# One set of weights for both directions in the mLSTM heads, and denominators from a product with ones

## The reference

```
w[t,s] = (q[t]·k[s]) * exp(log_d[t,s] - m[t])
num[t] = sum_s w[t,s] v[s]
den[t] = sum_s w[t,s]
h[t]   = num[t] / max(|den[t]|, exp(-m[t]))
```

```python
h = num / jnp.maximum(jnp.abs(den), jnp.exp(-m_t))[..., None]
...
return yc_f + jnp.flip(yc_b, axis=2), yl_f + jnp.flip(yl_b, axis=2)
...
y = from_heads(head_norm(h, LN_EPS, True)) * norm_g + skip * xc
return (y * jax.nn.silu(z.astype(jnp.float32))).astype(z.dtype)
```

## Time and profile before

| | us |
|---|---|
| median of 3 runs | 2862.51 |
| profiled execution | 2845.39 |
| its span | 2843.5 |
| heads: first product of scores to last gating | 2015.0 to 2613.6 |
| PE busy in the whole span | 2487.3 |
| DVE busy in the whole span | 1573.6 |

### The profile page before, as it was taken

How to read it: one execution, slowest core, us unless ns; L and a number is a source line. 1 busy time by engine, 2 the same in 40 slices (tenths; PEclk the granted TensorE clock), 3 DMA queues, 4 the chain that set the end, 5 groups by cost and what they waited for, 6 DMA issues and landing times. The chain is left out here.

```text
span 2843.5 us, 53344 instructions
## 1 busy us (share of the span) xinstructions
PE 2487.3 (87%) x22670; PEld 2117.7 (74%) x22670; DVE 1573.6 (55%) x2510; ACT 901.1 (32%) x1504; POOL 729.5 (26%) x689
## 2 busy tenths in 40 slices
PE   6899999995898986777959999999599999995986
PEld 2577776775877774666848888878499999995865
DVE  3026878644456545764665665566455656565233
ACT  2113344231232333555123333332443443431310
POOL 1111110115757642000222222221222222221421
PEclk8999999997999997889979999999799999997998
DMA  7712545545333324114543444443724443312521
GB/s 276 247 53 76 152 133 156 172 141 170 94 104 95 109 67 121 30 61 170 128 85 129 161 161 161 154 167 122 278 88 149 145 142 134 104 60 94 191 93 60
DMA packets 338235, 372.05 MB, mean 131 GB/s; under 512 B 111247, under 2 KB 274838, under 8 KB 335438
## 3 DMA queue, kind: packets, MB, share of 16 engines
q1 hardware_dynamic: 336992, 365.31, 40.1%
q10 hardware_dynamic: 1006, 3.33, 0.3%
HBM read 228.76 MB, written 139.82 MB: 130 GB/s over the span
## 5 line engine op out<-in xcount | busy, mean ns | idle before, releaser
L3338 PE MATMUL PS<-V_hi,weights_hi 128*128 128x258 f32 x832 | 238.2, 286 | 10.4 <-DVE H L3549 6.9
L469 PE MATMUL PS<-hT_hi,w_in_hi 128*128 128x512 f32 (+1 forms) x640 | 239.6, 374 | 4.4 <-DVE q_out L3137 4.4
L3339 PE MATMUL PS<-V_lo,weights_hi 128*128 128x258 f32 x832 | 237.0, 285 | 0.0
L470 PE MATMUL PS<-hT_lo,w_in_hi 128*128 128x512 f32 (+1 forms) x640 | 236.3, 369 | 0.0
L471 PE MATMUL PS<-hT_hi,w_in_lo 128*128 128x512 f32 (+1 forms) x640 | 236.2, 369 | 0.0
L3340 PE MATMUL PS<-V_hi,weights_lo 128*128 128x258 f32 x832 | 236.1, 284 | 0.0
L469 PE MATMUL PS<-h_hi,w_in_hi 128*128 128x512 f32 (+1 forms) x624 | 229.9, 368 | 5.8 <-PEq L115 3.7
L3446 POOL TENSOR_TENSOR weights_lo<-weights,weights_hi 128x1664 fp32r<-128x1664 f32 x32 | 122.0, 3813 | 413.1 <-ACT weights_hi L3398 413.1
L470 PE MATMUL PS<-h_lo,w_in_hi 128*128 128x512 f32 (+1 forms) x624 | 225.7, 362 | 0.0
L471 PE MATMUL PS<-h_hi,w_in_lo 128*128 128x512 f32 (+1 forms) x624 | 225.3, 361 | 0.0
L3310 PE MATMUL PS<-Q_hi,K_hi 128*128 128x256 f32 x640 | 184.7, 289 | 28.5 <-DVE weights L3515 13.4
(11 more groups left out here) (453 smaller groups left out, 6178.4 us busy)
## 6 DMA issues: line engine op xcount, KB each, us to landing
chunk_in<-in_d SPq DMA_DIRECT2D x40, 512.0 KB, 3.4
w_in<-in_e_w_in_dram SPq DMA_DIRECT2D x30, 512.0 KB, 5.0
xnew<-in_o_w_in_dram SPq DMA_DIRECT2D x30, 512.0 KB, 6.4
in_d<-xnat SPq DMA_DIRECT2D x20, 640.0 KB, 6.0
modw<-in_mod_w_dram SPq DMA_DIRECT2D x12, 1024.0 KB, 9.7
xnat<-in_mod_w_dram SPq DMA_DIRECT2D x8, 1536.0 KB, 7.2
v_d<-xnew SPq DMA_DIRECT2D x16, 640.0 KB, 2.9
kh_d<-k_hi SPq DMA_DIRECT2D x16, 640.0 KB, 2.9
```

The costliest lines, as they stand in the source:

```text
L469: pe.matmul(PS[:, bank + off // 512, 0:n], wh[:, k], hh[:, k, t], start=(k == 0), stop=False)
L470: pe.matmul(PS[:, bank + off // 512, 0:n], wh[:, k], hl[:, k, t], start=False, stop=False)
L3338: pe.matmul(out, wh, VH[:, j, q], start=(j == seen[0]), stop=False)
L3339: pe.matmul(out, wh, VL[:, j, q], start=False, stop=False)
```

## The change

- The 13 slots stay (`slot` orders them otherwise), and `weights` has three buffers in place of two. When both directions' weights of a tile are there, DVE sums each direction's slots (`sum_weights`, a reduction that reads with a step of one slot, 512 bytes, between elements).
- PE multiplies these sums with a matrix of ones (`den_sums`, fp32), which gives each direction's denominator, broadcast over all partitions, in a PSUM bank of its own.
- `merge(n)` on DVE takes the larger of |den| and exp(-m) for both directions (the rows exp(-m) come by a broadcast DMA, `least_rows`, issued by ACT from a new DRAM tensor F_d), scales the slots of the direction that sees fewer keys by the quotient, and adds the three slots that both see. Ten slots are left.
- `high`, POOL's low part and `values` work on ten slots; `values` takes all 512 columns in one product. One bank holds the sum, two are used in turn. ACT moves it to H unscaled (`evict`); the other direction's denominator is carried into the variance as eps times its square, before the root.
- The programs of ACT and DVE are written in a new order. On DVE a pair is now one piece.

```diff
-        W = sb("weights", [P, 2, SEEN, P])
+        W = sb("weights", [P, 3, SEEN, P])
...
+                def den_sums(n):
+                    c = n % TQ + CTXCH
+                    pe.wait_ge(s["summed"], n + 1)
+                    if n >= 2:
+                        pe.wait_ge(s["merged"], n - 1)
+                    pe.matmul(PS[:, 2 + n % 2, 0:2 * P], G.c("ones"), sums[:, n % 2].rearrange("p d t -> p (d t)"), start=True, stop=True)
+                    pe.matmul(PS[:, 2 + n % 2, 2 * P:2 * P + 1], sums[:, n % 2, 1 - minor(c)], G.c("ones")[:, 0:1],
+                              start=True, stop=True).then_inc(s["den_ps"], 1)
...
-                    if n:
-                        pe.wait_ge(s["av_sb"], n)
-                    for d in range(2):
-                        seen = uses(d, i + CTXCH)
-                        for j in seen:
-                            wh, wl = (x[n % 2][:, slot(d, i + CTXCH, j)] for x in (WH, WL))
-                            for half, q in enumerate((slice(0, 2 * P + 2), slice(2 * P + 2, 4 * P + 2))):
-                                out = PS[:, 2 * d + half, 0:q.stop - q.start]
-                                pe.matmul(out, wh, VH[:, j, q], start=(j == seen[0]), stop=False)
-                                pe.matmul(out, wh, VL[:, j, q], start=False, stop=False)
-                                last = pe.matmul(out, wl, VH[:, j, q], start=False, stop=(j == seen[-1]))
+                    if n >= 2:
+                        pe.wait_ge(s["h_ok"], n - 1)
+                    for j in range(NCH):
+                        wh, wl = (x[n % 2][:, merged_slot(c, j)] for x in (WH, WL))
+                        out = PS[:, n % 2, :]
+                        pe.matmul(out, wh, VH[:, j], start=(j == 0), stop=False)
+                        pe.matmul(out, wh, VL[:, j], start=False, stop=False)
+                        last = pe.matmul(out, wl, VH[:, j], start=False, stop=(j == NCH - 1))
...
+                    den_sums(2 * m)
+                    den_sums(2 * m + 1)
...
-                    high(n)
+                    if n + 2 < STEPS:
+                        decay(n + 2)
                     if i == 0 and h:
                         values(h)
-                    if n + 2 < STEPS:
-                        decay(n + 2)
-                    if i == 5:
+                    high(n)
+                    if n:
+                        evict(n - 1)
+                    if i == 4:
                         root(h, 0)
-                    if i == 1 and h:
+                    if i == 0 and h:
                         root(h - 1, 1)
+                evict(STEPS - 1)
...
+                def sum_weights(n):
...
+                    for d in range(2):
+                        last = dve.tensor_reduce(sums[:, n % 2, d], W[:, n % 3, span(d, c)].rearrange("p s t -> p t s"), AX, ALU.add)
+                    last.then_inc(s["summed"], 1)
...
+                def merge(n):
...
+                    step.add(dve.scalar_tensor_tensor(den[:, i:i + 1], col, -1.0, floor[:, 1 - b, c, h:h + 1], ALU.mult, ALU.max))
+                    step.link(dve.scalar_tensor_tensor(flow, row, -1.0, flow, ALU.mult, ALU.max))
+                    step.add(dve.tensor_tensor(den[:, i:i + 1], col, den[:, i:i + 1], ALU.max))
+                    step.link(dve.tensor_tensor(flow, row, flow, ALU.max))
+                    step.link(dve.reciprocal(low[:, b], low[:, b]))
+                    step.link(dve.tensor_tensor(low[:, b], low[:, b], low[:, 1 - b], ALU.mult))
+                    part = w[:, span(b, c)]
+                    step.link(dve.tensor_tensor(part, part, low[:, b][:, None, :].broadcast_to([P, part.shape[1], P]), ALU.mult))
+                    mine, other = w[:, NCH * (1 - b):NCH * (1 - b) + 3], w[:, NCH * b:NCH * b + 3]
+                    dve.tensor_tensor(mine, mine, other, ALU.add).then_inc(s["merged"], 1)
...
-                for n in range(STEPS):
-                    h, i, m = n // TQ, n % TQ, n // 2
-                    if i == 0 and h:
-                        low_values(dve, h)
-                    if m + 1 < PAIRS:
-                        weigh_groups(m + 1, range(EARLY) if n % 2 == 0 else range(EARLY, NG))
-                    if i == 5:
-                        normalize(h, 0)
-                    if i == 1 and h:
-                        normalize(h - 1, 1)
-                    if i == 3:
+                for m in range(PAIRS):
+                    h, i = m // PAIRS1, m % PAIRS1
+                    n0, n1 = 2 * m, 2 * m + 1
+                    sum_weights(n0)
+                    sum_weights(n1)
+                    if i == 2:
                         skip(2 * h)
                     if i == 0 and h:
                         skip(2 * h - 1)
-                    if i == 5:
+                    merge(n0)
+                    if i == 0 and h:
+                        low_values(dve, h)
+                    merge(n1)
+                    if m:
+                        collect(n0 - 1)
+                    if m + 1 < PAIRS:
+                        weigh_groups(m + 1, range(EARLY))
+                    if i == 2:
+                        normalize(h, 0)
+                    if i == 0 and h:
+                        normalize(h - 1, 1)
+                    collect(n0)
+                    if m + 1 < PAIRS:
+                        weigh_groups(m + 1, range(EARLY, NG))
+                    if i == 2:
                         take(h, 0)
-                    if i == 1 and h:
+                        finish(h, 0)
+                    if i == 0 and h:
                         take(h - 1, 1)
-                    collect(n)
-                    if n + 4 < STEPS:
-                        diag(n + 4)
-                    if i == 5:
-                        finish(h, 0)
-                    if i == 1 and h:
                         finish(h - 1, 1)
+                    for n in (n0 + 4, n1 + 4):
+                        if n < STEPS:
+                            diag(n)
+                collect(STEPS - 1)
```

More of the change, by code:

```diff
@@ L3157, in slot, with span, minor, merged_at @@
     def slot(d, c, j):
-        return j if d == 0 else c + 1 + (j if j < CTXCH else CTXCH + j - c)
+        both = [0, 1, c]
+        if j in both:
+            return both.index(j) + NCH * d
+        return j + 1 if d == 0 else j
+    def span(d, c):
+        return slice(0, c + 1) if d == 0 else slice(c + 1, SEEN)
+    def minor(c):
+        return 0 if c < NCH // 2 + 1 else 1
+    def merged_at(c):
+        return 3 if minor(c) == 0 else 0
+    def merged_slot(c, j):
+        return slot(1 - minor(c) if j in (0, 1, c) else (0 if j < c else 1), c, j) - merged_at(c)
     NG = NCH // 2
+    AX = mybir.AxisListType.X
     EARLY = 3
@@ L3368, in root @@
                 def root(h, half):
-                    act.wait_ge(s["mean_ok"], TQ * h + 4 * half + 4)
+                    act.wait_ge(s["spread"], 2 * h + half + 1)
                     t = slice(4 * half, 4 * half + 4)
-                    act.activation(rs[:, 0, t], mv[:, t, 1], ACT.Sqrt, bias=eps[:]).then_inc(s["root"], 1)
+                    act.activation(rs[:, 0, t], mv[:, t, 1], ACT.Sqrt).then_inc(s["root"], 1)
                 def decay(n):
@@ L3397, in high, with evict @@
                         act.wait_ge(s["w_lo"], n - 1)
-                    act.activation(WH[n % 2][:], W[:, n % 2], ACT.Copy).then_inc(s["w_hi"], 1)
+                    act.activation(WH[n % 2][:], W[:, n % 3, at:at + NCH], ACT.Copy).then_inc(s["w_hi"], 1)
+                    if n + 2 < STEPS:
+                        least_rows(n + 2)
+                def evict(n):
+                    h, i = n // TQ, n % TQ
+                    act.wait_ge(s["av_ps"], n + 1)
+                    if h and i % 4 == 0:
+                        act.wait_ge(s["turned"], 8 * (h - 1) + i + 4)
+                    act.activation(H[:, i], PS[:, n % 2, :], ACT.Copy).then_inc(s["h_ok"], 1)
                 def values(h):
@@ L3416, in _ @@
                     act.activation(gx[64:68, t], ga[64:68, u], ACT.Copy).then_inc(s["ga_ok"], 1)
+                act.wait_ge(s["rows_ok"], 3)
+                for d in range(2):
+                    q = slice(64 * d + 32, 64 * d + 36)
+                    act.activation(gl[q, CTX:], gx[q, CTX:], ACT.Exp).then_inc(s["f_ok"], 1)
                 values(0)
@@ L3512, in weigh @@
                         js = [j for j in uses(d, c) if 2 * g <= j < 2 * g + 2]
-                        if js:
-                            w = W[:, n % 2, slot(d, c, js[0]):slot(d, c, js[0]) + len(js)]
-                            last = dve.tensor_tensor(w, src[:, js[0] - 2 * g:js[-1] + 1 - 2 * g, a], w, ALU.mult)
+                        at = [slot(d, c, j) for j in js]
+                        if len(js) == 2 and at[1] != at[0] + 1:
+                            runs = [(js[:1], at[0]), (js[1:], at[1])]
+                        else:
+                            runs = [(js, at[0])] if js else []
+                        for keys, first in runs:
```

(36 more changed lines are left out.)

66 lines of the change are left out of this document (37 added, 29 removed).

## The result

The changed kernel takes 2909.6 us (median; before in the same comparison 2861.4): ratio 1.0182, interval 1.0148 to 1.0216, **48 us slower**. The forecast was slower, 2892 us. Earlier stages, whose code is the same, end at different times in the profiles: the heads start at 2015 us in the one of before and at 2022 to 2037 in the others. So I compare the heads: from the first score to the last transposes 591.7 us before (2015.0 to 2606.7) and 647.0 after (2036.8 to 2683.9), +55.3 us. Why the medians differ by 7 us less stays open.

The account below looks back on a forecast made before the run. PE was taken as the bound: -70.7 saved in pairs, +50.4 and +46.2 at turns, +8.2 start, -4.8 end make +29.3 us, 2874.7 against the profile, 2892 as median. Own range 2876 to 2915 (0.62); 8 in 10, 2858 to 2948.

Parts of the forecast that it names:

- PE is bound, 4.4 us less a pair: All sixteen pairs: PE sets the pace and its work falls from 33.1 to 28.7 us a pair, -70.7 us in all.
- the product with ones: PE's fp32 denominator product: 0.35 us a tile with its small companion, bounds 0.12 and 0.6.
- The turn: Pairs with a turn: PE idles 7.2 and 1.3 us for sums, restarts at half clock (1.9); +50.4 us (i == 2), +46.2 (i == 0).
- Sums of 2.0 us a tile: DVE's two reductions of a tile's weights take 2.0 us, bounds 1.1 and 3.5.
- Waits inside the pair (2.2 us): Pair with a turn: fifth score group finds its bank late, and POOL's low parts come late; 2.2 us.
- the hold: DVE's second merge is held some 2.3 us at its 128x128 product, beside POOL's low part.
- The low values, 3.9 us: Turns with i == 0: PE waits 3.9 us for the new head's low values, which stand between DVE's two merges.
- Start and end: Start of the heads: PE idles 4.3 and 1.3 us at the first sums, +8.2 us in all; end: -4.8 us.
- A plain pair, "cost 0": Pair without a turn: DVE's 6.1 us up to the sums hide under PE's 6.8 us of values; cost 0.
- Rival 1: Sums pay for their step: 1.94 ns an element, 3.5 us a tile, all pairs lose; 2942 to 2954 us; chance 0.20.
- Rival 2: Cheap sums of 1.1 us a tile and no hold by POOL: 2863 us, no change; chance 0.08.
- Rival 3: PE stays the bound, with sums ready soon after a turn: 73 us less, 2819 us; chance 0.10 for 2819 to 2855.

Follow-up runs that it names:

- e7: e1's kernel with each sum reading only the first key tile of its span, so denominators are other numbers: 2808.9 us, ratio to before 0.9831.
- e10: Changed kernel with 66 added PE products behind each of seven turns and ten more between the two tiles' ones products: 2897.5 us, ratio 1.0130.
- e1: Changed kernel with a turn's take moved behind the next pair's two sums on DVE, and finish behind its second merge: 2849.8 us, ratio to before 0.9977.
- e2: Changed kernel with sums reading the same bytes at a step of 4 bytes, not 512, so denominators sum other elements: 2883.5 us, ratio 1.0089.
- e4: Changed kernel with DVE's two merges of a pair parted by the previous tile's statistics and the even tile's early weighting: 2906.2 us, ratio 1.0182.
- e5: Changed kernel with each sum over key tiles made by unit-step additions that halve the tiles, in place of one strided reduction: 2896.1 us, ratio 1.0128.
- e3: Changed kernel with 56 added products of 252 columns on PE behind each of seven turns: 2909.0 us, ratio 1.0185.

## Why the prediction was right in direction, and where it fell short

The measured 2909.6 us lies in the forecast's own range, 2876 to 2915. That range was made from the bounds of the reciprocal, the products with ones and the waits inside the pair; what moved the time most, the size of the sums, was not among them.

- **PE is bound, 4.4 us less a pair.** The mechanism was right; e7 shows 3.7. The step of 512 columns was as read, 0.23 us (five from 2177.76 to 2178.91), not the 131 ns of the Trainium skill ("TensorE: Matmul & The Clock Gate", "Back-to-back issue gap"). The term that was mis-sized is the product with ones: 0.67 us a tile (two instructions) in place of 0.35, over its bound of 0.6; 32 x 0.32 = 10 us. That is worked out; no run changed these products. The row that the forecast took had the sign in it: L1499 has 24 instructions (16 of 512 columns, 8 of 256) where the program makes 12 products.
- **The turn.** The step "PE idles 7.2 us, then 1.3, then restarts at half clock for 1.9" measured 7.8, 1.3 and 1.4 to 1.7 (e10). The second wait is right by luck: the second tile's sums end 2.73 us after the first's, not 2.0, and the products with ones between them, at half clock, take 1.44 us, not 0.7. e1 shows that the written order of DVE is the cause: 60 us.
- **Sums of 2.0 us a tile.** This size failed: 3.1 us, within the bounds of 1.1 and 3.5. The rate and the fixed part were right for a unit step (e2: 2.0 us a tile), and the step of 512 bytes is what they lacked. e2 prices that: 26 us by the medians, 28 in the heads. Its heads take 618.6 us (2029.0 to 2647.6), 26.9 more than before, where the forecast had +29.3. So the size of the sums explains all of the 26 us by which the heads (+55.3) missed the forecast, and the other errors nearly cancel.
- **Waits inside the pair (2.2 us) and the hold.** This mechanism failed. In the pairs with i == 2 no score product waits for its bank, and the value products wait 0.24 and 0.22 us:
```profile
2159.09 0.47 PE L3370 MATMUL PS<-V_hi,weights_hi 128*128 128x512 f32 x1 [0.24 <-issue]
...
2172.18 0.47 PE L3370 MATMUL PS<-V_hi,weights_hi 128*128 128x512 f32 x1 [0.22 <-issue]
```
That is 0.5 in place of 2.2 us, four times, some 7 us too much. The hold was there (up to 2.55 us), but e4 shows it cost nothing in this kernel. In e2, whose sums have the forecast's size, a turn with i == 2 and the pair behind it lose (38.0 - 31.2) + (33.2 - 29.4) = 10.6 us against e7, forecast 12.6; one with i == 0 loses 15.3, forecast 17.8. These 15 us too much hid the 10 us too little of the products with ones. Some 3 us are left over, for start, end and what I did not measure apart.
- **The low values, 3.9 us.** Right: three waits, 12.0 us (L3370 <- V_lo above).
- **Start and end.** PE idled 4.88 and 1.44 us at the first products with ones, forecast 4.3 and 1.3. At the end it waits 6.42 us at 2662.94 us, where GpSimd's low part of the last pair's first tile ends at 2662.84.
- **A plain pair, "cost 0".** 30.4 us against 29.4 in e2, e5 and e7: its second tile's sums are late by about 1 us.
```profile
2149.31 0.70 PE L3353 MATMUL PS<-weight_sums,cst 128*128 128x256 f32 x2 [1.05 <-DVE weight_sums L3597]
```
Two signs that I had named for a failure did come: a plain pair over 30 us, and reductions over 1.6 us (all of more than 768 elements, up to 2.37). DVE's busy time in the heads grew by 137 us (339.0 to 475.6), not by some 100.
- **Rival 1** had the rate right (1.94 ns said, 1.99 measured) and the price wrong: 2942 to 2954 supposed 3.0 us lost in every pair, and outside the turns it is about 1. **Rival 2** falls with the rate; its second half, the hold, gives nothing in e4. **Rival 3** is what e1 built: it moves 5.2 of the 6.1 us that stood in the chain, and the change gains. The place was priced at 73 us; this part of it measured 60.

## What to carry to other kernels

When a change lets PE wait for something that DVE makes at the end of a stage, look first at what stands ahead of it in DVE's written order: here 5.2 us of work that nobody needed yet cost 60 us, more than the change could give. Where such a wait ends on a reduction over a strided axis, try a tree of unit-step additions: it gave 14 and 19 us here. Price an fp32 product by its number of instructions, and repeat in the best version a test that gave nothing, since a longer wait can hide what it would show.

## What the runs showed of the hardware

- A DVE sum over a step of 512 bytes costs 1.99 ns an element, over 4 bytes 1.04. That agrees in direction with the Trainium skill's "Advanced Engine Details and Errata", "SBUF Cachelines"; the runs try only these two steps.
- An fp32 product with 256 columns is two instructions, 0.67 us with its one-column companion at full clock (e10, 2176.52 to 2177.19) and about 1.3 at half.
- A single wait of 1.53 us left the clock at 1.00 (e1). Waits of 1.33 and 1.92 us with one tile's products with ones between them were followed by 0.55 (e3), a wait of 7.77 us by 0.50 for about 7.7 us. The same two places with waits of 0.26 and 0.73 us kept 1.00 (e10).
- A reciprocal of 128 elements takes 954 ns; for one element it was 154, so 6.3 ns on average for each further one.
